# The two mixers of a fused two-block model: own normalised copy of x dropped, attention spread between the convolution's projections

## The chip, the cores and the metric

One core of a Trainium2 chip runs the whole model. The metric is the time of one execution in microseconds on the device. The engines named below are TensorE (PE), VectorE (DVE), ScalarE (ACT), GpSimd (POOL) and SyncE (SP), which issues most DMAs.

## The reference, cut to what matters

x is 256 tokens by 1024 channels, all in float32. The model runs eleven stages: mixer, mixture of experts, mixer, mixture of experts, a norm, two feed-forward stages with a pooling mixer between, a feed-forward stage, a sparse-attention mixer ("nsa") and a last feed-forward stage. Only the two mixers change. Each computes:

```
h    = rmsnorm(x, norm_mix)
proj = h @ w_in                      # 1024 -> 512 q, 128 k, 128 v, 512 gate_b, 512 gate_c, 512 u
q, k = partial_rope(q), partial_rope(k)                  # 8 query heads, 2 key/value heads, width 64
y_attn = windowed_gqa_with_sink(q, k, v, sink)           # keys with |i-j| <= 128, one sink logit per head
y_conv = gate_b * centred_short_conv(gate_c * u, conv_w) # 3 taps over the tokens
y = concat(rmsnorm(y_attn, g_attn), rmsnorm(y_conv, g_conv))
x = x + y @ w_out
```

## The kernel before

All engines run one hand-written program; the order of the work is the order of the statements, and semaphores join the engines. The weights stream through a ring of six 2 MB buffers in SBUF. SP issues the loads in the order in which they are used, and each waits until its buffer's last user has signalled. A mixer uses seven buffers (five column blocks of `w_in`, two row blocks of `w_out`), and the ring then fills with the first six expert matrices. In the expert stage a load is issued when the pair of experts before has been multiplied (L516).

A mixer on PE (`mixer`, from L771): turn the normalised `hp` into `hT` (`transpose_h`, L693) and wait for all of it; q, k and v with tokens on the partitions (`tokens_out`, L704); gate_c, u and gate_b with channels on the partitions (`channels_out`, L718), 96 matmuls in a row; turn q and k (L783, L786); then four attention units, two blocks of 128 queries by two key/value heads, in `attend`: scores of 4 heads by 256 keys (L731), turning the probabilities (L743), the product with V (L754), where the turned probabilities are the stationary operand and 64 columns of V move. Then the sums of squares of the convolution's output (L795), its half of the out-projection (L814), turning the attention's output (L803), and the other half (L814).

ACT takes results from PSUM (`copy`, L1240), takes the exponentials (L1327) and the roots. DVE normalises x into `hp` (`norm`, L1647), rotates q and k (L1714 to L1718), makes the convolution (L1785 to L1800), adds the window's mask to the scores in SBUF (L1730), takes their maximum (L1732) and three small steps (L1738 to L1742), scales each head's output (L1807), and adds the two halves to x (L1821). In the nsa stage the kernel already has an attention with the mask added on PE (L1130), two heads of a pair on the two halves of the rows (L1135), probabilities scaled by DVE before they are turned (L2153, L1150), and V stationary (L1160).

Of the kernel before, what the change touches and what calls it, by code (L numbers as in the profile page):

```python
# [14 lines left out]
P = 128  # L15
# [30 lines left out]
for _n, _w in (("ident", P), ("upper", P), ("ones", P), ("fold", CAP), ("iota", CAP), ("tie", NG + NE), ("rope_c", TT * ROPE),  # L46
               ("rope_s", TT * ROPE), ("band", TT * SEQ), ("causal", P), ("cmp_mask", TT * NCMP), ("cmp_any", TT)):
    CONSTS[_n] = (_at, _at + _w)
    _at += _w
# [3 lines left out]
def constants():  # L53
# [20 lines left out]
    keys = np.arange(SEQ)  # L74
    put("band", np.where(np.abs(keys[None, None, :] - tok[:, :, None]) <= 128, 0.0, -BIG))
# [15 lines left out]


class Unit:


    def __init__(self, t, g, half, gp, tile, br, nk, qT, kT, v, mask):
        self.t, self.g, self.half, self.gp, self.tile, self.br, self.nk = t, g, half, gp, tile, br, nk
        self.qT, self.kT, self.v, self.mask = qT, kT, v, mask
# [39 lines left out]
def build(nc, a, out, stages):  # L138
    ctx = ExitStack()
    with ctx:  # L140
# [54 lines left out]
        r_query = small[:, 28:30]  # L195

# [41 lines left out]
        S.masked = sem("masked")  # L238
# [3 lines left out]
        S.turned_taken = sem("turned_taken")  # L242
        S.valued = sem("valued")
        S.o_taken = sem("o_taken")
        S.conv_gain = sem("conv_gain")
        S.conv_ss = sem("conv_ss")
        S.conv_root = sem("conv_root")
        S.ya_root = sem("ya_root")
        S.ya_psum = sem("ya_psum")
        S.yaT_ready = sem("yaT_ready")  # L250
        S.acc_done = sem("acc_done")
# [69 lines left out]
        def mixer_views():  # L321
            c = Carve()
            b = Fields()
            b.q, b.kv = c(TT, 512), c(TT, 256)
            b.v = b.kv[:, :, P:256]
            b.qT, b.kT = c(4, SEQ), c(1, SEQ)
            b.ya, b.yc = c(TT, 512), c(4, SEQ)
            b.tmp = c(256)
            b.stat = c(4, 16)
            b.z = c(4, SEQ + 2)  # L330
            b.P = [c(4, SEQ) for _ in range(2)]
            b.Sm = [c(4, SEQ) for _ in range(2)]
            b.PT = [c(2, 4, P) for _ in range(2)]
            b.sq = hp[:, 0, :].rearrange("p (a b) -> p a b", a=4)
            b.gate_c = hp[:, 1, :].rearrange("p (a b) -> p a b", a=4)
            b.cv = b.P[0]
            b.yaT = b.Sm[0]
            b.junk = b.Sm[1]
            return b
# [83 lines left out]
        def mixer_units():  # L423
            return [Unit(t=t, g=g, half=g, gp=0, tile=0, br=0, nk=2, qT=MB.qT, kT=MB.kT, v=MB.v,
                                    mask=const("band")[:, t * SEQ:(t + 1) * SEQ])
                    for t in range(TT) for g in range(2)]
# [40 lines left out]
        def _(sp):  # L467
# [153 lines left out]
        def _(pool):  # L621
# [6 lines left out]
            with nc.allow_non_contiguous_dma(reason="small parameters, transposed"):  # L628
# [8 lines left out]
                par(gT[:, 0, :], a["norm_mix"][0].rearrange("(p k) -> p k", k=KT), True)  # L637
# [8 lines left out]
                par(gT[:, 1, :], a["norm_mix"][1].rearrange("(p k) -> p k", k=KT))  # L646
# [26 lines left out]
        def _(pe):  # L673
# [25 lines left out]
            def tokens_out(r, width, banks, offs=(0, 0), each=True):  # L699

                wv = view(r, KT, width)
                for t in range(TT):
                    for k in range(KT):
                        last = pe.matmul(PS[:, banks[t], offs[t]:offs[t] + width], hT[:, k, t * P:(t + 1) * P],  # L704
                                         wv[:, k, :], start=(k == 0), stop=(k == KT - 1))
                    if each:
                        last.then_inc(S.projected, 1)
                if not each:
                    last.then_inc(S.projected, 1)

            def channels_out(r, banks):

                wv = view(r, KT, 512)
                for c in range(4):
                    if c == 2 and banks[1] == 4:
                        pe.wait_ge(S.act_took, w.to(S.act_took))
                    for k in range(KT):
                        last = pe.matmul(PS[:, banks[c // 2], (c % 2) * SEQ:(c % 2 + 1) * SEQ],  # L718
# [5 lines left out]
            def attend(units, b):  # L724
                def scores(i):
                    u = units[i]
                    if i >= 2:
                        pe.wait_ge(S.masked, w.to(S.masked))
                    lo = DH * u.half
                    for r in range(4):  # L730
                        last = pe.matmul(PS[:, 2 * (i % 2) + r // 2, (r % 2) * SEQ:(r % 2) * SEQ + u.nk * P],  # L731
                                         u.qT[lo:lo + DH, u.tile + r, u.t * P:(u.t + 1) * P],
                                         u.kT[lo:lo + DH, u.gp, 0:u.nk * P], start=True, stop=True)
                    last.then_inc(S.scored, 1)

                def turn(i):
                    u = units[i]
                    pe.wait_ge(S.exped, w.to(S.exped))
                    if i:
                        pe.wait_ge(S.turned_taken, w.to(S.turned_taken))  # L740
                    for kt in range(u.nk):
                        for r in range(4):
                            last = pe.transpose(PS[:, 4 + kt, r * P:(r + 1) * P],  # L743
                                                b.P[i % 2][:, r, kt * P:(kt + 1) * P], ident)
                    last.then_inc(S.turned, 1)

                def values(i):
                    u = units[i]
                    if i >= 2:
                        pe.wait_ge(S.o_taken, w.to(S.o_taken))  # L750
                    for r in range(4):
                        lo = r * DH
                        for kt in range(u.nk):
                            last = pe.matmul(PS[:, 6 + i % 2, lo:lo + DH], b.PT[i % 2][:, kt, r, :],  # L754
                                             u.v[:, kt, u.g * DH:(u.g + 1) * DH],
                                             start=(kt == 0), stop=(kt == u.nk - 1))
                    last.then_inc(S.valued, 1)

                scores(0)
                for i in range(len(units)):  # L760
                    if i + 1 < len(units):
                        scores(i + 1)
                    turn(i)
                    if i:
                        values(i - 1)
                pe.wait_ge(S.turned_taken, w.to(S.turned_taken))
                values(len(units) - 1)
                pe.wait_ge(S.masked, w.to(S.masked, 2))
                pe.wait_ge(S.o_taken, w.to(S.o_taken, 2))

            def mixer(l):  # L771
                transpose_h()
# [1494 lines left out]
```

## Time and profile before

| | us |
|---|---|
| three runs | 2336.04, 4395.04, 2329.59; median 2336.04 |
| the profiled execution | 2328.93, of which the trace spans 2327.1 |
| PE busy | 2145.3 (92%) |
| DVE busy, ACT busy | 767.1 (33%), 630.8 (27%) |
| chain that ended last | PE 65%, DMA 27%, DVE 5%, ACT 2% |

The profile's page gives each engine's busy time and follows back the chain of work that ended last; the trace behind it gives every instruction. The two mixers lie at about 9 to 164 us and 665 to 822 us of the span. Busy time of PE is modelled and holds short matmuls' fill, so it isn't a share of PE's peak. A float32 matmul stands as two instructions in the trace (x64 for 32 matmuls of L704); a transpose is one.

### The profile page before, as it was taken

To read this page: it belongs to the slowest core of one execution; us is meant where nothing else is said; L and a number is where in the kernel's file an instruction comes from. 1 tells how busy PE (TensorE), PEld (TensorE's weight loads), DVE (VectorE), ACT (ScalarE), POOL (GpSimd) and SP (SyncE) were. 2 spreads that over 40 slices of the span, in tenths; PEclk is the share of its full clock that TensorE was granted. 3 is DMA by queue.
4 is the path that set the end of the run, shared out by engine and by line. 5 is a ranking of instruction groups with operands and counts; after the bars stand their busy time and mean duration, and the time that the engine had idled before them with its cause. 6 is when DMAs were issued, how large, how long until landed. Compare 5 with 4: busy or idle time off the path is not lost.

```text
span 2327.1 us, 28410 instructions
## 1 busy us (share of the span) xinstructions
PE 2145.3 (92%) x11998; PEld 1469.0 (63%) x11998; DVE 767.1 (33%) x1119; ACT 630.8 (27%) x886; POOL 35.9 (2%) x53
## 2 busy tenths in 40 slices
PE   6889999999978989999999799989999999999998
PEld 4755443444437644444444499969998995566997
DVE  1321111111112221111111365555556553274555
ACT  1221111111111211111111333343344332264333
POOL 5000000000000000000000000000000000000000
PEclk9879999999989789999999899989999999999999
DMA  9326999999964149999999955354455435513430
GB/s 282 156 72 266 421 422 421 422 421 422 422 242 175 36 171 422 421 422 421 423 422 421 395 181 181 114 209 164 174 201 203 162 130 176 179 56 144 167 125 36
DMA packets 142459, 599.18 MB, mean 257 GB/s; under 512 B 6913, under 2 KB 22337, under 8 KB 126002
## 3 DMA queue, kind: packets, MB, share of 16 engines
q1 hardware_dynamic: 139730, 592.27, 65.1%
q0 software_dynamic: 2656, 5.86, 1.0%
q8 instruction: 55, 0.90, 0.2%
q14 instruction: 18, 0.15, 0.0%
HBM read 597.06 MB, written 1.05 MB: 257 GB/s over the span
## 4 chain that ended last, share of the span: by engine, by line
PE 65%; DMA 27%; DVE 5%; ACT 2%; issue 1%; SPq 0%; DVEq 0%; ACTq 0%
DMA ring<-in_w_expert_up 26%; PE PS L972 20%; PE PS L848 12%; PE PS L986 10%; PE PS L718 4%; PE PS L1059 3%; PE PS L814 3%; PE PS L959 2%; PE PS L704 2%; PE PS L859 1%; PE PS L1212 1%; PE PS L837 1%; PE PS L754 1%; DMA ring<-in_w_in 1%; PE PS L731 1%
## 5 line engine op out<-in xcount | busy, mean ns | idle before, releaser
L848 PE MATMUL PS<-ring,xs 128*64 128x512 f32 x2048 | 465.6, 609 | 57.1 <-DMA ring<-in_w_expert_up 55.7
L848 PEld LDWEIGHTS PS<-ring,xs 128*64 128x64 f32 x2048 | 159.8, 140 | 356.3 <-issue 353.3
L1240 ACT ACTIVATE split<-ring 128x2048 fp32r<-128x2048 f32 x132 | 253.1, 1920 | 424.2 <-PE PS L972 268.0
L1693 DVE TENSOR_TENSOR split<-ring,split 128x2048 fp32r<-128x2048 f32 x132 | 302.3, 2293 | 176.9 <-ACT split L1240 171.7
L972 PE MATMUL PS<-hT_high,split 128*128 128x256 f32 x2560 | 329.1, 281 | 0.0
L972 PEld LDWEIGHTS PS<-hT_high,split 128*128 128x128 f32 x2560 | 316.5, 189 | 2.8
L986 PE MATMUL PS<-split,ffn_hid 128*128 128x512 f32 x1056 | 246.9, 390 | 0.0
L859 PE MATMUL PS<-ring,work 128*64 128x512 f32 x1024 | 226.8, 595 | 0.0
L986 PEld LDWEIGHTS PS<-split,ffn_hid 128*128 128x128 f32 x1056 | 195.5, 188 | 39.0
L972 PE MATMUL PS<-hT_low,split 128*128 128x256 f32 x1280 | 178.3, 282 | 0.0
L1240 ACT ACTIVATE work<-PS 128x512 f32<-128x512 f32 (+1 forms) x73 | 47.4, 656 | 439.5 <-PE PS L884 326.6
L972 PEld LDWEIGHTS PS<-hT_low,split 128*128 128x128 f32 x1280 | 163.6, 189 | 0.0
L1854 DVE SCALAR_TENSOR_TENSOR y_low<-PS,work,y_high 128x1024 fp32r<-128x1024 f32 x32 | 41.1, 1284 | 353.7 <-ACT y_high L1393 353.7
L1849 DVE TENSOR_TENSOR work<-PS,work 128x512 f32<-128x512 f32 x32 | 22.1, 691 | 410.8 <-PE PS L848 410.8
L859 PEld LDWEIGHTS PS<-ring,work 128*64 128x64 f32 x1024 | 70.7, 137 | 131.8 <-issue 127.9
L837 PE MATMUL PS<-work,hp 128*128 128x128 f32 x1088 | 132.6, 282 | 3.0 <-DVE work L1831 3.0
L837 PEld LDWEIGHTS PS<-work,hp 128*128 128x128 f32 x1088 | 129.6, 199 | 3.2 <-issue 3.2
L1393 ACT ACTIVATE y_high<-PS,work 128x1024 fp32r<-128x1024 f32 x32 | 35.6, 1113 | 207.7 <-PE PS L859 207.7
L718 PE MATMUL PS<-hT,ring 128*128 128x256 f32 x384 | 83.2, 379 | 0.0
L718 PEld LDWEIGHTS PS<-hT,ring 128*128 128x128 f32 x384 | 73.0, 190 | 9.9
L1240 ACT ACTIVATE xs<-PS 128x512 f32<-128x512 f32 x68 | 40.6, 597 | 130.0 <-PE PS L837 130.0
L1059 PE MATMUL PS<-ring,hT 128*128 128x512 f32 (+1 forms) x192 | 72.9, 539 | 0.4 <-ACT hT L1501 0.4
(265 smaller groups left out, 1680.3 us busy)
## 6 DMA issues: line engine op xcount, KB each, us to landing
ring<-in_w_expert_gate SPq DMA_DIRECT2D x64, 2048.0 KB, 17.4
ring<-in_w_expert_up SPq DMA_DIRECT2D x64, 2048.0 KB, 17.7
ring<-in_w_expert_down SPq DMA_DIRECT2D x64, 2048.0 KB, 14.4
ring<-in_ffn_w_gate SPq DMA_DIRECT2D x20, 2048.0 KB, 8.7
ring<-in_ffn_w_up SPq DMA_DIRECT2D x20, 2048.0 KB, 9.1
ring<-in_ffn_w_down SPq DMA_DIRECT2D x20, 2048.0 KB, 7.9
ring<-in_w_in SPq DMA_DIRECT2D x8, 2048.0 KB, 18.9
ring<-in_nsa_w_in SPq DMA_DIRECT2D x5, 2048.0 KB, 7.9
```

Source lines behind the costliest of these rows:

```text
L704: last = pe.matmul(PS[:, banks[t], offs[t]:offs[t] + width], hT[:, k, t * P:(t + 1) * P], wv[:, k, :], start=(k == 0), stop=(k == KT - 1))
L718: last = pe.matmul(PS[:, banks[c // 2], (c % 2) * SEQ:(c % 2 + 1) * SEQ], wv[:, k, c * P:(c + 1) * P], hT[:, k, :], start=(k == 0), stop=( ...
L814: last = pe.matmul(PS[:, 4 * part + 2 * t + h, :], src[:, c, t * P:(t + 1) * P], wv[:, c, h * 512:(h + 1) * 512], start=(c == 0), stop=(c ...
L837: last = pe.matmul(PS[:, 6 + b, (k % 4) * P:(k % 4 + 1) * P], hp[:, t, k * P:(k + 1) * P], EB.OH[:, t, :], start=(t == 0), stop=(t == 1))
L848: last = pe.matmul(PS[e * CAP:(e + 1) * CAP, bank, :], xs[:, k, e * CAP:(e + 1) * CAP], view((r + e) % RING, KT, DE)[:, k, :], start=(k == ...
L859: last = pe.matmul(PS[e * CAP:(e + 1) * CAP, 6 + c, :], EB.hT[:, k, e * CAP:(e + 1) * CAP], view((r + e) % RING, 4, D)[:, k, c * 512:(c + ...
L959: last = pe.matmul(PS[:, 2 * (kind == "up") + ft, 0:SEQ], split_cols(0, kind, part)[:, k, ft * P:(ft + 1) * P], hx[:, k, :], start=(n_ == ...
L972: last = pe.matmul(PS[:, bank, ft * SEQ:(ft + 1) * SEQ], split_cols(b, kind, part)[:, k, ft * P:(ft + 1) * P], hx[:, k, :], start=(n_ == 0 ...
L986: last = pe.matmul(PS[:, 2 * t + c, :], ffn_hid[:, b % 2, hpart, ft, t * P:(t + 1) * P], wv[:, ft, c * 512:(c + 1) * 512], start=(b == 0 a ...
L1059: last = pe.matmul(PS[:, banks[t], offs[t]:offs[t] + width], hT[:, k, t * P:(t + 1) * P], wv[:, k, :], start=(k == 0), stop=(k == KT - 1))
L1240: return act.activation(o, i, ACT.Copy)
L1693: v.tensor_tensor(at[:, 1], src, at[:, 0], ALU.subtract).then_inc(S.ffn_low, 1)
```

## The change

- No normalised copy: PE turns x itself (`transpose_x`, which the expert stage has too, here with its line in the first mixer waiting for the load of x), hT holds x times the gain, and the root of the mean square comes in later: as a scale when ACT takes q, k and v, as a broadcast row `r2` (two matmuls of a diagonal with ones) on gate_c, and as one factor of the convolution's norm. u and gate_b are left without it.
- `w_in` is read with channels k*128+p on partition p instead of 8p+k, and `norm_mix` likewise. The mask table leaves the constants (512 of 1284 columns). 
- The first projection starts when the first two channel blocks of hT are there.
- k is taken twice, so that two query heads of a pair lie on the upper and lower 64 partitions; the mask comes from PE as a product of an identity with a triangle that opens the sum; the scale 1/8 is in q.
- Probabilities are divided by their sum on DVE before they are turned; ACT and DVE each take one half of the turned ones; V is stationary, and the output comes out turned, [64 x head, queries], straight usable by the out-projection. Its gain is applied when ACT takes it. The turning of the attention's output is gone.
- PE's order is new: the attention's units stand between the channel blocks of u and gate_b, and the out-projection is four pieces of 8 matmuls. The last ring slots of `w_out` are given back at the third and fourth piece.

The instructions that compute 4 sums of squares (L768 in the new program) are 16 matmuls instead of 8.

On PE, between the projection of k and v and the out-projection, before:

```order
L718 MATMUL PS<-hT,ring 128x256 x96
L783 MATMUL PS<-cst,work 128x128 x8
L786 MATMUL PS<-cst,work 128x128 x2
L731 MATMUL PS<-work 128x256 x8
L743 MATMUL PS<-cst,work 128x128 x8
L731 MATMUL PS<-work 128x256 x4
L743 MATMUL PS<-cst,work 128x128 x8
L754 MATMUL PS<-work 128x64 x8
```

And on the same engine in the changed program, from the second half of gate_c on (L723 channel blocks, L736 mask, L740 scores, L750 turning, L762 values):

```order
L723 MATMUL PS<-hT,ring 128x256 x16
L736 MATMUL PS<-causal_r,ident_r 128x2x128 x2
L740 MATMUL PS<-work 128x256 x4
L723 MATMUL PS<-hT,ring 128x256 x16
L750 MATMUL PS<-cst,work 128x128 x8
L736 MATMUL PS<-causal_r,ident_r 128x2x128 x2
L740 MATMUL PS<-work 128x256 x4
L723 MATMUL PS<-hT,ring 128x256 x8
L762 MATMUL PS<-work 64x256 x4
L723 MATMUL PS<-hT,ring 128x256 x8
L750 MATMUL PS<-cst,work 128x128 x8
```

All 96 channel matmuls stood ahead of the first score; now 64 of them stand between a unit's scores and its turning, 16 for each unit.

On DVE in the changed program, unit 1 with the work that stands around it (L1826 maximum, L1810 and L1815 convolution, L1843 scaling of the probabilities, L1804 the product gate_c*u, L1848 half of the turned probabilities):

```order
L1826 TENSOR_REDUCE work<-PS 128x4
L1829 TENSOR_TENSOR work<-work 128x4
L1832 TENSOR_TENSOR work<-work,sink 128x4
L1810 TENSOR_SCALAR work<-work,cw 128x256 x2
L1815 SCALAR_TENSOR_TENSOR work<-work,cw 128x256 x4
L1839 TENSOR_TENSOR work<-work 128x4
L1663 RECIPROCAL work<-work 128x4
L1843 TENSOR_TENSOR work<-work 128x1024
L1804 TENSOR_TENSOR work<-PS,work 128x2x256
L1848 COPY work<-PS 128x512
```

The convolution stood ahead of the attention; now half of it stands between the maximum and the scaling of units 1 and 2.

At the end of the mixer on PE, in the changed program (L774 out-projection, L768 sums of squares):

```order
L750 MATMUL PS<-cst,work 128x128 x8
L774 MATMUL PS<-ring,work 128x512 x8
L762 MATMUL PS<-work 64x256 x4
L768 MATMUL PS<-cst,work 128x1 x12
L774 MATMUL PS<-ring,work 128x512 x8
L768 MATMUL PS<-cst,work 128x1 x4
L774 MATMUL PS<-ring,work 128x512 x16
```

Before, 16 matmuls of L814, the 8 transposes of L803 and 16 of L814 stood there; the first piece now runs ahead of the last unit's values.

The diff, cut to the parts that the prediction speaks of:

```diff
@@ def mixer_loads(l) (SP)
-                    wide(wi, lo, hi, S.projected, k)
-                rows(a["w_out"][l], 512, 1024, S.acc_done, 1)
-                rows(a["w_out"][l], 0, 512, S.y_done, TT)
+                    wide(wi, lo, hi, S.projected, k, "(k p) n -> p k n")
+                rows(a["w_out"][l], 512, 1024, S.y_done, 3)
+                rows(a["w_out"][l], 0, 512, S.y_done, 1)
@@ PE
+            def mixer(l):
...
+                def scores(i):
+                    t, g = units[i]
+                    if i:
+                        pe.wait_ge(S.exped, w.to(S.exped))
+                    for h in range(2):
+                        other = PS[:, h, :].rearrange("p (s k) -> p s k", s=2)[:, :, (1 - t) * P:(2 - t) * P]
+                        kept, moved = (causal_r, ident_r) if t else (ident_r, causal_r)
+                        pe.matmul(other, kept[:, :], moved[:, :].unsqueeze(1).to_broadcast([P, 2, P]),
+                                  start=True, stop=False, skip_group_check=True)
+                    for s_ in range(2):
+                        for h in range(2):
+                            last = pe.matmul(PS[:, h, s_ * SEQ:(s_ + 1) * SEQ],
+                                             MB.qT[DH * h:DH * (h + 1), 2 * g + s_, t * P:(t + 1) * P],
+                                             MB.kT[DH * h:DH * (h + 1), g, :],
+                                             start=False, stop=True, skip_group_check=True)
+                    last.then_inc(S.scored, 1)
...
+                def values(i):
+                    t, g = units[i]
+                    pe.wait_ge(S.turned_act, w.to(S.turned_act))
+                    pe.wait_ge(S.turned_dve, w.to(S.turned_dve))
+                    if i >= 2:
+                        pe.wait_ge(S.oT_taken, w.to(S.oT_taken))
+                    for kt in range(TT):
+                        for h in range(2):
+                            last = pe.matmul(PS[DH * h:DH * (h + 1), 6 + g, 0:SEQ], MB.v[:, kt, g * DH:(g + 1) * DH],
+                                             MB.PT[i % 2][:, kt, 2 * h:2 * h + 2, :], start=(kt == 0), stop=(kt == 1))
+                    last.then_inc(S.oT_done, 1)
...
+                transpose_x(f"mix{l}", 4)
+                project(512, (0, 1), first=True)
+                project(256, (2, 2), (0, 256))
+                pe.wait_ge(S.diag_made, w.to(S.diag_made))
+                for t in range(TT):
+                    last = pe.matmul(PS[:, 6, t * P:(t + 1) * P], ones, MB.sF[:, t, :], start=True, stop=True)
+                last.then_inc(S.r_wide, 1)
+                wv = view(slot(), KT, 512)
+                channels(wv, 3, 0)
+                channels(wv, 3, 1)
+                pe.wait_ge(S.q_roped, w.to(S.q_roped, 3))
...
+                scores(0)
+                wv = view(slot(), KT, 512)
+                pe.wait_ge(S.gated, w.to(S.gated))
+                channels(wv, 3, 0)
+                channels(wv, 3, 1)
+                turn(0)
+                scores(1)
+                pe.wait_ge(S.gated, w.to(S.gated))
+                channels(wv, 2, 2)
+                pe.wait_ge(S.r_taken, w.to(S.r_taken))
+                values(0)
+                channels(wv, 2, 3)
+                turn(1)
+                scores(2)
...
+                rows_out(MB.oT, attn_w, 0, 0)
+                values(3)
+                pe.wait_ge(S.yc_gain, w.to(S.yc_gain, 2))
+                for t in range(TT):
+                    sum_squares(PS[:, 4, t:t + 1], MB.sqc, t)
+                sum_squares(PS[:, 4, 2:3], MB.sqa, 0).then_inc(S.mix_ss, 1)
+                rows_out(MB.yg, conv_w, 0, 2)
+                pe.wait_ge(S.oT_taken, w.to(S.oT_taken, 2))
+                sum_squares(PS[:, 5, 0:1], MB.sqa, 1).then_inc(S.mix_ss, 1)
+                rows_out(MB.yg, conv_w, 1, 6)
+                pe.wait_ge(S.mix_root, w.to(S.mix_root, 2))
+                rows_out(MB.oT, attn_w, 1, 4)
@@ ACT
+                exps(0)
+                for i in range(3):
+                    take(i)
+                    exps(i + 1)
+                    outputs(i)
+                table_for_roots()
+                conv_gain(0)
+                take(3)
+                conv_gain(1)
+                outputs(3)
```

## Rows read from the trace of the kernel before

**Rows 1.** Chain of waits, first mixer: start us, us, what
```profile
1.74 19.82 DMA ring<-in_w_in
21.70 22.46 PE PS L704 x64
44.16 41.44 PE PS L718 x192
...
126.85 3.55 PE PS L795 x16
130.40 15.75 PE PS L814 x32
...
148.24 14.02 PE PS L814 x32
162.35 1.29 DVE x L1821
```

**Rows 2.** Busy us by stretch: PE, PEld, DVE, ACT, POOL, granted clock, DMA share, GB/s
```profile
60.00:80.00 20.00, 20.00 (x94) 17.62 (x93) 7.36 (x15) 0.00 (x0) 0.00 (x0) 1.00 0.76 306
100.00:120.00 20.00, 18.84 (x75) 16.49 (x73) 7.40 (x16) 6.96 (x21) 0.00 (x0) 0.50 0.01 1
```

**Rows 3.** SP's issues in order of time, end of the first mixer
```profile
146.18 16.47 SPq L482 DMA_DIRECT2D ring<-in_w_expert_down  x2
194.29 0.92 SPq L516 DMA_DIRECT2D ring<-in_w_expert_gate  x2
```

**Rows 4.** Chain of waits, end of the first expert stage and second mixer
```profile
613.72 22.15 DMA ring<-in_w_expert_up
...
662.82 2.37 DVE x L1869 x2
...
681.42 20.88 PE PS L704 x64
...
806.49 14.02 PE PS L814 x32
```

**Rows 5.** PE in order of time, start of the second mixer and of ffn00
```profile
672.53 0.69 PE L693 MATMUL PS<-cst,hp 128*128 128x128 f32 x2 [9.75 <-issue]
677.18 3.22 PE L693 MATMUL PS<-cst,hp 128*128 128x128 f32 x14 [3.96 <-issue]
...
1329.49 3.67 PE L826 MATMUL PS<-cst,x 128*128 128x128 f32 x16 [9.49 <-DVE x L2232]
```

**Rows 6.** DMA queues from 669 to 670 us: packets, MB, share
```profile
q8 instruction: 1, 0.02, 7.1%
```

**Rows 7.** Instructions in order of time, first mixer
```profile
107.07 3.78 PE L731 MATMUL PS<-work 64*128 64x256 f32 x8
112.15 1.22 DVE L1732 TENSOR_REDUCE work<-work 128x4 f32<-128x1024 f32 x1
113.60 0.17 DVE L1740 TENSOR_SCALAR work<-work 128x4 f32<-128x4 f32 x1
...
145.99 1.04 PE L803 MATMUL PS<-cst,work 128*128 128x128 f32 x8
```

**Rows 8.** Groups by line and shape, first mixer: busy us, mean ns, idle before
```profile
L1327 ACT ACTIVATE work<-work 128x256 f32<-128x256 f32 x16 | 7.9, 493 | 0.0
L1795 DVE SCALAR_TENSOR_TENSOR work<-work,cw 128x256 f32<-128x256 f32 x8 | 3.9, 484 | 0.3
```

**Rows 9.** Instructions in order of time, nsa stage
```profile
2055.53 0.48 PE L1130 MATMUL PS<-causal_r,ident_r 128*128 128x256 f32 x2
2055.94 0.71 PE L1135 MATMUL PS<-work 64*128 64x128 f32 x8
...
2059.42 0.65 PE L1160 MATMUL PS<-work 128*64 128x256 f32 x4
```

**Rows 10.** Groups by line and shape, nsa stage
```profile
L2153 DVE TENSOR_TENSOR work<-work 128x1024 f32<-128x1024 f32 x8 | 9.8, 1224 | 0.3
```

**Rows 11.** Busy us by stretch, nsa attention (columns as in rows 2)
```profile
2050.00:2070.00 20.00, 20.00 (x146) 13.13 (x146) 13.01 (x28) 16.57 (x73) 0.00 (x0) 0.94 0.00 1
```

More of the change, by code:

```diff
@@ L423, in mixer_units, with mixer_scores @@
         def mixer_units():
[L424 to L426 removed]
+            return [(t, g) for t in range(TT) for g in range(2)]
+        def mixer_scores():
+            return PS[:, 0:2, :].rearrange("p h (s k) -> p (h s) k", s=2)
         def nsa_units():
@@ L697, in transpose_h @@
                 pe.wait_ge(S.hT_odd, w.to(S.hT_odd, 2))
[L699 to L718, printed above, removed]
-                                         wv[:, k, c * P:(c + 1) * P], hT[:, k, :],
-                                         start=(k == 0), stop=(k == KT - 1))
-                    if c % 2:
-                        last.then_inc(S.projected, 1)
@@ L724, in attend @@
[L724 to L769, printed above, removed]
@@ L1240, in copy @@
                 return act.activation(o, i, ACT.Copy)
-            def squares(src, junk, sums):
-                for t in range(TT):
-                    last = act.activation(junk(t), src(t), ACT.Square, accum_out=sums[:, t:t + 1])
-                last.then_inc(S.act_step, 1)
-                act.wait_ge(S.act_step, w.to(S.act_step))
             def roots(o, i, width, s):
@@ new lines, in take, with outputs @@
+                    copy(MB.PT[i % 2][:, 0, :, :].rearrange("p r q -> p (r q)"), PS[:, 4, :]).then_inc(S.turned_act, 1)
+                def outputs(i):
+                    t, g = units[i]
+                    act.wait_ge(S.oT_done, w.to(S.oT_done))
+                    o = PS[:, 6 + g, 0:SEQ].rearrange("p (s q) -> p s q", s=2)
+                    act.activation(MB.sqa[:, 2 * g:2 * g + 2, t * P:(t + 1) * P], o, ACT.Square)
+                    for s_ in range(2):
+                        m = 2 * g + s_
+                        last = act.activation(MB.oT[:, m, t * P:(t + 1) * P], o[:, s_, :], ACT.Copy, scale=gaT[:, l, m:m + 1])
+                    last.then_inc(S.oT_taken, 1)
@@ new lines, in conv_gain @@
+                def conv_gain(half):
+                    act.wait_ge(S.yc_made, w.to(S.yc_made))
+                    act.activation(MB.sqc[:, 2 * half:2 * half + 2, :], MB.yc[:, 2 * half:2 * half + 2, :], ACT.Square)
+                    for c in range(2 * half, 2 * half + 2):
+                        last = act.activation(MB.yg[:, c, :], MB.yc[:, c, :], ACT.Copy, scale=gcT[:, l, c:c + 1])
+                    last.then_inc(S.yc_gain, 1)
+                exps(0)
[3 more added lines that the diff above has]
+                    outputs(i)
@@ L1377, in experts @@
+                roots(root_mix[:, 3:4], PS[:, 5, 0:1], 512, S.mix_root)
             def experts(s, f, passes, y_high):
@@ L1771, in mixer @@
+                for t in range(TT):
+                    last = v.tensor_scalar(MB.sF[:, t, :], ident, rstd[:, t:t + 1], rstd[:, t:t + 1], ALU.mult, ALU.mult)
+                last.then_inc(S.diag_made, 1)
                 for t in range(TT):
```

480 lines of the change are left out of this document (257 added, 223 removed).

## Prediction, made before the changed kernel ran

> **What bounds the kernel now.** I read the chain of waits first. In the first mixer it is PE almost without a break: it waits for the first block of `w_in` until 21.6 us, projects q, k and v in 22.46 us, runs 96 channel matmuls in 41.44, and ends with two halves of the out-projection, 15.75 and 14.02 us [rows 1]. The second mixer has the same chain from 681.42 to 820.51 us [rows 4]. Between the last channel matmul (85.60 us) and the out-projection (130.40) lie 44.8 us of attention and sums of squares. Here the stretches show what is wrong: the granted clock is 1.00 in the projections and 0.50 from 100 to 120 us, although PE counts as busy for 18.84 of 20 us there [rows 2]. So attention costs twice: PE waits for DVE and ACT between a unit's scores and its turning, and its matmuls then run at 1.2 instead of 2.4 GHz.
>
> Does time saved in a mixer reach the end? The expert stage between is bound by its loads (one of 22.15 us is a link of the chain [rows 4]), and a stage bound by DMA can swallow a gain on PE. But its steady loading begins at 194.29 us, 30.6 us after x is ready at 163.64, since it waits for the first pair of experts to be multiplied [rows 1, 3], and in the mixer's late part DMA is idle (share 0.01 [rows 2]). An earlier x shifts that whole stream, so the gain carries over one for one.
>
> **The change, part by part.** I sum the PE work of the changed mixer from its first projection to its last matmul, at full clock.
>
> - q, k, v: unchanged, 20.88 us (second mixer [rows 4]; 22.46 in the first, where PE starts from idle [rows 1]).
> - 96 channel matmuls, only moved: 41.44 us [rows 1]. Out-projection, unchanged in size: 2 x 14.02 = 28.0.
> - 12 transposes of q and k: 8 took 1.04 us [rows 7], so 1.6. The two matmuls for `r2`, four instructions of that width: 0.5.
> - Sums of squares, now 16 matmuls of one column. Before, 8 took 3.55 us [rows 1] just before the out-projection still began slow. At full clock I take half of that each: 3.6 for 16. Upper bound 7.1.
> - One unit: mask 0.48; scores 8 instructions of 128 columns in 0.71 us in nsa, where the two heads of a pair lie on different rows of PE, so 1.4 for 256 columns (upper bound 1.9, half of the 3.78 us that this mixer's unpaired scores took at half clock); turning 1.04; values 0.65 for half of them, so 1.3 [rows 7, 9]. Together 4.2, four units 16.8.
>
> The sum is 20.9 + 41.4 + 28.0 + 1.6 + 0.5 + 3.6 + 16.8 = 112.8 us, and 1.6 more in the first mixer. Before, that stretch was 140.6 us (21.70 to 162.26) and 139.1 us. Gain: 26.2 and 26.3 us.
>
> This holds if PE does not wait for a unit's softmax. What must fit under the channel matmuls: maximum 1.22, two small steps 0.34, then on DVE half of the convolution, four steps of 0.48 and two shorter, some 2.6, in which ACT takes its four exponentials (4 x 0.49 and 0.2), then two small steps 0.35 and the scaling 1.22: 5.8 us [rows 7, 8, 10]. PE has 16 channel matmuls there, 41.44 / 6 = 6.9 us, and for units 1 to 3 another 1.3 of values. The cover is thin for unit 0, but that one has no convolution in its way (5.3 us). Each later unit has over 2 us to spare. If the cover were gone, a unit would expose the whole 5.8.
>
> ACT's copies of q, k and v with a scale and the rotation of the now doubled k lie under the first eight gate_c blocks (6.9 us). Square and gain of the convolution, the last take and the table of roots on ACT lie under the first out-projection piece (7.0 us), where only the last unit's take is waited for. DVE's adds lie under the later pieces; the last one, 1.29 us, stays exposed as before [rows 1]. So these cost nothing; with the cover gone they are at most some 4 us a mixer. The two last ring buffers return later relative to the end (at the third and fourth piece instead of halves one and two). They feed the first pair's down matrices, and the first pair's gate loads are used up only 30.6 us after x, so there is room for two loads.
>
> Front of the first mixer: it stays bound by the load of `w_in`. Norm, transposes and hT are done ahead of it before and now. The constants shrink by 512 of 1284 columns, 256 KB ahead of that load, at the first stretch's pace about 1 us; the new row order of `w_in` keeps pieces of 2 KB. I take 0.8 (0 to 1.2). The parameters' gather of `norm_mix` in single floats could take some of it back.
>
> Front of the second mixer: here a norm of both row blocks, transposes of `hp` and a wait for all of hT disappear, and x is ready at 665.19 while the projection starts at 681.42 [rows 4]. In ffn00, which turns x itself, 16 transposes take 3.67 us, and the first products follow at once [rows 5]. That would give a start at about 668, a gain of 13 us. But PE did not stand still for data alone: it ran two transposes at 672.53, stopped for 3.96 us with nothing to wait for, and ran on at 677.18 [rows 5], and a packet of instructions was brought in at 669 to 670 us [rows 6], just after the branch over the unused expert code. If both stops remain in time, the 14 last transposes end at 680.4 and the gain is 1.0; if only the first, the projection starts at about 676.4 and it is 5. I take 3, with 0 and 13 as the ends.
>
> The Trainium skill (Runtime: NRT & Kernel Launch, "Instruction fetch mechanics") says that a taken branch to code outside the resident pages must wait for a DMA fetch. By that rule the stops belong to the jump and not to the norm, which agrees with the row on the packet; without it the sum would have 10 us more gain.
>
> **Sum:** 26.2 + 26.3 + 0.8 + 3 = 56.3 us off the profiled 2328.93: 2272.6. The profiled execution lies 7 us under the shown median (2336.04) and 0.7 under the lowest run, so I put the median at 2272.
>
> **The rivals.**
>
> *A. The softmax is exposed.* DVE and ACT answer later than PE works through 16 channel matmuls. Before, they were exposed in every unit, which speaks for it; the sum of 5.8 under 6.9 to 8.2 us speaks against, and so does nsa, where the same pieces keep PE at 20.00 of 20 us [rows 11]. All four units exposed in both mixers cost 8 x 5.8 = 46 us: 2319.
>
> *B. The clock stays down, and the kernel gets slower.* The stretch at 0.50 had PE counted busy for 94% [rows 2], so short matmuls with many weight loads do not by themselves bring the clock back. If the mixture of units and channel blocks is seen like that, it is the dense work that pays: from the first scores to the end PE has 16.8 + 27.6 + 3.6 + 28.0 = 76 us a mixer. At half clock that is 152 us more in all, 96 net: 2425. If the clock came back at the out-projection it would be 89 us more, 32 net: 2361. The gain is gone at 28 us a mixer at 1.2 GHz; slower by 2% needs 52 of the 76. Against it: nsa's attention, with turned probabilities, paired heads and V stationary, had 0.94 [rows 11], and 64 dense channel matmuls now stand between.
>
> The Trainium skill (TensorE: Matmul & The Clock Gate, "A second HAM failure mode: psum-queue depth-cycling") describes a kernel that rests briefly between groups while it cycles through PSUM banks and whose clock swings between both levels. The nsa row does not bear that out for these pieces, and no row shows it for this mixture.
>
> *C. The front of the second mixer gains all of it:* 13 instead of 3, 2262.
>
> *D. The gain doesn't arrive,* because the expert stage's loads set its end whatever x does: both mixers' gains but the front's would have to be hidden in it, and I have found no row for it: about 2325.
>
> **Chances.** A measurement of this kernel can tell about 2% (47 us, 2289) from no change. Forecast 0.71, C 0.11, A 0.10 in full or in most part, B 0.05 (0.03 at 2425), D 0.03. The forecast's own range is 2262 to 2284: unknown prices are 3.5 us a mixer for the sums of squares, 2 for the scores, a few us of handovers, and the front. For 8 in 10 I reach from C's 2257 to a part of A, 2292. Faster by over 2%: forecast, C and a piece of A, 0.84. Within 2%: 0.12. Slower by over 2%: 0.04.
>
> **What would show each step.** The chain in a mixer should be channel, mask, score and value matmuls on PE with no DVE or ACT link over 1 us between. The granted clock from the first projection to the last matmul should be near 1.00. The out-projection should be four pieces of 7.0 us. From the first projection to the last matmul it should be 111 to 118 us. The steady expert loads should begin near 163 us. A stop "issue" on PE at the second mixer's first transposes should remain. I am wrong if PE waits for the scaled probabilities by more than 2 us a unit, if the clock shows 0.5 to 0.8 between, or if the expert stages, 501 us from x to x, change length.

## The result and the profile after

The changed kernel took 2272.56 us (median of four, 2270.97 to 2273.72), the kernel before 2332.82 on the same chip: a ratio of 0.9754 with an interval of 0.9737 to 0.9770, faster by 2.5%. One of the four executions of the kernel before took 4395.04 us, and the ratio leaves it out, so it stands for 57 us where the two medians lie 60 apart. The forecast was 2272, and the profiled execution took 2272.86, with a span of 2271.0 against 2327.1. The spans differ by 56.1 us; the prediction's sum had 56.3.

The chain of waits in the first mixer after (start us, us, what). It answers to [rows 1].

```profile
60.56 0.23 PE PS L736 x2
60.79 1.06 PE PS L740 x8
61.86 7.10 PE PS L723 x32
68.96 0.87 PE PS L750 x8
...
100.44 0.87 PE PS L750 x8
101.31 6.87 PE PS L774 x16
108.18 1.01 PE PS L762 x8
109.19 2.77 PE PS L768 x24
111.96 8.67 PE PS L774 x16
120.63 0.79 PE PS L768 x8
121.42 13.86 PE PS L774 x32
```

All of it is PE: mask (L736), scores (L740), channel matmuls (L723), turning (L750), values (L762), sums of squares (L768), out-projection (L774). Where 44.8 us of attention stood before, no DVE or ACT link is left. The chain at the start of the second mixer after answers to [rows 4, 5]:

```profile
635.24 2.37 DVE x L1936 x2
...
638.59 6.22 issue
644.81 2.82 PE PS L697 x12
647.63 1.83 issue
649.46 0.66 PE PS L697 x4
```

and the same chain at the end of that mixer:

```profile
734.97 3.28 PE PS L768 x24
738.25 9.83 PE PS L774 x16
748.08 0.79 PE PS L768 x8
748.87 13.86 PE PS L774 x32
```

The norm, the transposes of `hp` and the wait for hT are gone, but the two stops of [rows 5] are there again: PE waits 6.22 and 1.83 us with nothing that the profile shows. Last, the stretches after (busy us of PE, PEld, DVE, ACT and POOL, granted clock, DMA share, GB/s), to be held against [rows 2]:

```profile
80.00:100.00 20.00, 20.00 (x110) 15.70 (x109) 10.84 (x22) 9.29 (x30) 0.00 (x0) 1.00 0.29 106
100.00:120.00 20.00, 20.00 (x74) 10.62 (x73) 3.00 (x5) 4.12 (x12) 0.00 (x0) 0.91 0.29 105
740.00:760.00 20.00, 20.00 (x50) 9.21 (x49) 3.48 (x4) 1.41 (x3) 0.00 (x0) 0.90 0.15 43
```

PE is busy for all 20 us of each, and the clock is 1.00 while units and channel blocks alternate (also from 60 to 80 us). Between the first projection and the last matmul it falls only at the sums of squares (109.19 and 734.97): it is 0.57 from 112 to 116 us, just behind them, and 0.84 from 735 to 738, while they run.

**Where the 56.1 us came from.** From the first projection to the last matmul it is 114.1 us in the first mixer (21.16 to 135.28) and 112.6 in the second (650.12 to 762.73), against 140.6 and 139.1: 26.5 us each. The first mixer starts 0.5 us earlier. In the second, the way from x to the projection fell from 16.2 to 12.5 us (637.61 to 650.12): 3.7. Those make 57.2. The expert stage between took 500.95 us from x to x against 501.55, so it passed on everything and 0.6 more, 57.8 us in all at the last add of the second mixer (764.11 against 821.89); its steady loads follow x, now at 166.6 us instead of 194.29 [rows 3]. The issues after, by line and operation (ns shortest/median/longest, first and last start in us):

```profile
L506 SPq DMA_DIRECT2D ring<-in_w_expert_gate x8: 345/346/363, 166.6 to 248.8; - x8
```

At the end of the second expert stage the kernel was 57.1 us ahead (1322.41 against 1265.32), at the end of the span 56.1; I did not follow these last 1.7 us.

### The profile page after: what moved, and what is told of

Same layout as the page of the kernel before. It is cut to its first block, busy times and chain, and to the rows that moved or that the text cites. A ratio compares the mean times of both kernels' runs of the same rounds, so it can differ in the third digit from the quotient of the medians.

```text
span 2271.0 us, 28397 instructions
## 1 busy us (share of the span) xinstructions
PE 2110.4 (93%) x11978; PEld 1432.7 (63%) x11978; DVE 769.3 (34%) x1125; ACT 628.4 (28%) x902; POOL 35.7 (2%) x53
## 4 chain that ended last, share of the span: by engine, by line
PE 65%; DMA 28%; DVE 4%; issue 1%; ACT 1%; SPq 0%; DVEq 0%; ACTq 0%
DMA ring<-in_w_expert_up 27%; PE PS L987 20%; PE PS L863 12%; PE PS L1001 10%; PE PS L723 4%; PE PS L1074 3%; PE PS L774 3%; PE PS L974 2%; PE PS L713 2%; PE PS L874 1%; PE PS L1227 1%; PE PS L852 1%; DMA ring<-in_w_in 1%; DVE x L1701 1%; PE PS L697 1%
## 5 line engine op out<-in xcount | busy, mean ns | idle before, releaser
L1921 DVE SCALAR_TENSOR_TENSOR y_low<-PS,work,y_high 128x1024 fp32r<-128x1024 f32 x32 | 41.1, 1284 | 353.7 <-ACT y_high L1425 353.7
L1255 ACT ACTIVATE work<-PS 128x512 f32<-128x512 f32 (+1 forms) x65 | 40.0, 619 | 370.5 <-PE PS L899 325.2
L723 PE MATMUL PS<-hT,ring 128*128 128x256 f32 x384 | 87.3, 383 | 0.0
L723 PEld LDWEIGHTS PS<-hT,ring 128*128 128x128 f32 x384 | 71.5, 190 | 14.0 <-issue 5.0
## 6 DMA issues: line engine op xcount, KB each, us to landing
ring<-in_w_expert_gate SPq DMA_DIRECT2D x64, 2048.0 KB, 17.4
```

Of the source, the lines that this page charges most:

```text
L723: last = pe.matmul(PS[:, bank, (c % 2) * SEQ:(c % 2 + 1) * SEQ], wv[:, k, c * P:(c + 1) * P], hT[:, k, :], start=(k == 0), stop=(k == KT - 1))
L1255: return act.activation(o, i, ACT.Copy)
```

## The experiments

There were three theories: (1) most of the gain is PE working through channel blocks while DVE and ACT do a unit's softmax, and the granted clock staying up with it; (2) what is left at the second mixer's start is the fetch of code behind the branch over the unused expert code; (3) the slow out-projection piece comes from the one-column matmuls ahead of it. The kernel before, on the chips of these runs, lay between 2328.47 and 2332.95 us, so small differences are read from traces or on one chip.

**e1: the units after the channel blocks.** The change's pieces are all kept, but the four units no longer alternate with the blocks. ACT and DVE are reordered to match.

```diff
-                scores(0)
...
-                turn(0)
-                scores(1)
...
-                values(0)
...
+                scores(0)
+                pe.wait_ge(S.yc_made, w.to(S.yc_made, 2))
+                for i in range(4):
+                    if i + 1 < 4:
+                        scores(i + 1)
+                    turn(i)
+                    if i:
+                        values(i - 1)
+                values(3)
```

> The changed kernel with its cheap attention units, but all 96 channel matmuls ahead of the first score, and the units in the old two-deep order (next scores, turn, values of the one before); ACT and DVE reordered to match. Theory (half of the gain or more is the spreading: it hides the softmax and keeps the clock up): the granted clock falls to about 0.5 in the attention, a unit takes 6 to 7 us instead of 3.2, the sums of squares double; some 22 us more a mixer, about 2317. Rival (the gain comes from the dropped work: no copy of x, paired heads, V stationary, no turning of the output; order is worth little): at most 5 us a mixer, 2282 or less.

Measured: 2303.5 us, ratio 0.9874 (0.9854 to 0.9894), against 0.9754 for the change. Its chain in the first mixer:

```profile
87.30 1.24 DVE work L1833
...
89.16 1.83 ACT work L1368 x8
...
91.42 1.24 DVE work L1850
...
92.70 1.97 PE PS L753 x8
...
95.10 2.03 PE PS L740 x8
```

and its stretches:

```profile
80.00:100.00 20.00, 13.16 (x66) 10.25 (x64) 8.66 (x17) 5.74 (x25) 0.00 (x0) 0.80 0.30 106
100.00:120.00 20.00, 15.94 (x72) 9.82 (x73) 6.89 (x13) 9.51 (x29) 0.00 (x0) 0.69 0.00 1
```

The DVE and ACT links are back on the chain, and turning (L753) takes 1.97 us instead of 0.87, since the clock is at its lower level there. The mixers last 128.9 and 130.0 us: 14.8 and 17.4 longer than after, 11.7 and 9.1 shorter than before. So alternation is worth about half of the gain: 28 of 57 us by the ratios, 32 of 53 by the mixers of these executions. Theory (some 2317) gave it too much and the rival (2282 or less) too little.

The first mixer's chain also parts the two prices. In one block the four units take 31.8 us (85.96 to 117.78) against 12.7 when they alternate, 19.1 more. PE's own links are 17.6 of the 31.8, so the lower clock is some 4.9 of the 19.1, and the other 14.2 are waits for DVE and ACT. Channel matmuls in one row, a faster first projection and faster out-projection pieces gave 4.3 us back.

The first mixer of e1 is 11.7 us shorter than that of the kernel before. The stretch from the first score to the last value fell from 38.4 us (87.49 to 125.88) to 31.8, the turning of the output (2.1) is gone, and the out-projection took 27.9 instead of 29.8. Those are 10.6 of the 11.7. The single pieces (mask on PE, row halves, stationary V) were not taken out one by one.

**e2: two score matmuls on the same rows of PE next to each other.** Does the price of the scores rest on the order in which the two halves are written?

```diff
-                    for s_ in range(2):
-                        for h in range(2):
+                    for h in range(2):
+                        for s_ in range(2):
```

> The four score matmuls of a unit in the order h, s instead of s, h, so that matmuls that follow each other use the same half of PE's rows. Theory (neighbouring heads on different row halves run beside each other): a unit's scores take 1.8 us instead of 1.06, all on PE's path, 8 x 0.75 = 6 us more, about 2278.5. Rival (PE pairs them whatever the order, or the pair does not overlap): no change, 2272.5.

Measured: 2272.82 us, ratio 0.9744 (0.9728 to 0.9761). The eight instructions took as long as before the edit:

```profile
58.02 1.07 PE PS L740 x8
```

The order is worth nothing. This does not show that the two halves are worth nothing: in both orders one unit's scores use both. At the lower clock these eight took 2.03 us in e1, and the old kernel's eight of the same shape, all four matmuls of a unit on one half of the rows, 3.78 [rows 7].

**e3: no branch.** The overflow body of the expert stage, which these inputs never need, is left out with its test on PE, ACT, DVE and SP.

```diff
-                pe.wait_ge(S.flag_ready, w.to(S.flag_ready))
                 pe.wait_ge(S.moe_added, w.to(S.moe_added))
-                most = pe.value_load(flag[0:1, l:l + 1], min_val=0, max_val=SEQ)
-                with pe.If(most > CAP):
-                    experts(OV[l], Follow(), MORE * PAIRS, y_high[l])
...
```

> Leaves out, on all engines, the read of the flag and the branch with the second expert passes behind it, which these inputs do not enter. Theory (the 6.22 us and 1.83 us in which PE stands at the second mixer's first transposes come from the jump over that code): PE starts them within 1 us of x, the first projection some 8 to 10 us earlier; in the norm after the second expert stage PE has other work to wait for, so little there; about 2262. Rival (PE stands there for another reason, such as the busy DMA queues or x itself): gain under 1.5 us, 2271 to 2272.

Measured: 2260.25 us, ratio 0.9692 (0.9676 to 0.9708). The chain at its second mixer:

```profile
637.31 2.82 PE PS L696 x16
640.13 21.51 PE PS L712 x64
```

The 16 transposes run at once, and the projection starts 3.1 us after x (636.99) instead of 12.5. Both stops went with the branch and the code behind it; together with what they cover they cost 9.4 us. The edit takes out both at once, so it does not say which of the two a stop belongs to; e4 and e7 do. The time fell by 12.3, and the difference is theory 3's: in this execution the second mixer's slow piece took 6.97 us instead of 9.83, and the sums ahead of it 2.77 instead of 3.28.

**e4: PE waits for the sums of x behind the branch.** Then the branch does not stand behind DVE's last adds.

```diff
-                pe.wait_ge(S.moe_added, w.to(S.moe_added))
+                added = w.to(S.moe_added)
                 most = pe.value_load(flag[0:1, l:l + 1], min_val=0, max_val=SEQ)
                 with pe.If(most > CAP):
+                    pe.wait_ge(S.moe_added, added)
                     experts(OV[l], Follow(), MORE * PAIRS, y_high[l])
```

> PE waits for the sums of the expert stage (the DVE adds, S.moe_added) inside the branch's fall-through path instead of ahead of the branch. Theory (the stop of 6.22 us at the second mixer is the fetch of the code behind the branch, and it starts only once PE has waited for the last add): the fetch starts some 2.4 us earlier, beside the last DVE link of 2.4 us, so the stop after x is ready is near 3.9 us instead of 6.22, the second mixer ends about 2.4 us earlier and the time is near 2270. Rival (the stop starts with the wait inside the new code, or the sequencer reaches the branch no earlier than x is ready): no change, 2272.5.

Measured: 2268.79 us, ratio 0.9735 (0.9718 to 0.9752), which overlaps the change's interval. In the profiled execution (2272.34 us) the pieces behind the sums of squares took 9.91 and 9.95 us, so a gain at the front would not show in its time. The chain decides:

```profile
637.09 2.37 DVE x L1937 x2
...
640.45 0.25 issue
640.70 2.82 PE PS L697 x12
643.52 3.21 issue
646.73 0.66 PE PS L697 x4
```

The first stop is gone under DVE's work: transposes start 1.2 us after x (639.46) instead of 7.2. Part of it came back at once, since the second stop grew from 1.83 to 3.21 us. From x to the projection it is 7.9 us, 4.6 less than after, twice the 2.4 that I expected. The queue that brings in instructions says why. Its packets, from 642 to 643 us after, then from 638 to 639 and from 644 to 645 us in e4:

```profile
q8 instruction: 1, 0.02, 6.7%
q8 instruction: 1, 0.02, 6.9%
q8 instruction: 1, 0.02, 7.3%
```

After, the first packet comes some 5 us behind x (637.61). In e4 it comes some 1 us ahead of x (639.46), so the fetch no longer waited for the adds. A second packet lies ahead of the end of each second stop too (from 646 to 647 us after, where PE goes on at 649.46), and e3 has none between 626 and 654 us. This is the row of [rows 6] again, and it bears out that both stops are fetches of code.

**e7: the same code, moved.** 30 or 64 waits, never executed, are written into the overflow body of the first expert stage.

```diff
                 with pe.If(most > CAP):
+                    if l == 0:
+                        for _ in range(30):
+                            pe.wait_ge(S.const_loaded, 16)
                     experts(OV[l], Follow(), MORE * PAIRS, y_high[l])
```

> 30 waits are written on PE into the overflow body of expert stage 0, which is never executed; all code of PE behind the branch moves to higher addresses. Nothing that is executed changes. Theory (the two stops of PE at the start of the second mixer, 6.22 us before the transposes and 1.83 us after 12 of them, lie where the fetch of code ends a piece of fixed size): the second stop comes at another transpose, not after the 12th, and the projection begins up to 2 us later or earlier than 650.12. Rival (the second stop is a wait on data or a semaphore): it stays after the 12th transpose, with the same 1.8 us.

> As e7_pad30, with 64 waits. Theory (fetch in pieces of fixed size): the second stop comes at a third place or is gone, and the projection begins at another time than in both others, some 1.5 us earlier than 650.12 if the stop is gone. Rival (data or a semaphore): the second stop stays after the 12th transpose, with 1.8 us.

The chains, with 30:

```profile
635.36 6.20 issue
641.55 1.11 PE PS L697 x4
642.67 3.43 issue
646.10 2.82 PE PS L697 x12
```

and with 64:

```profile
639.81 6.22 issue
646.02 3.67 PE PS L697 x16
```

Nothing that is executed differs, and the second stop comes after 4 transposes instead of 12, or not at all. It is no wait for data: its place depends on where the code lies. From x to the projection it is 14.6 and 10.9 us, against 12.5. The first stop is the same in all three, 6.20 to 6.22 us. The times of one execution each, 2273.83 and 2268.58 us, point the same way, but single times do not settle 2 us.

**e5: the sums over channel blocks on DVE.** PE keeps one one-column matmul per sum instead of four.

```diff
-                def sum_squares(to, src, t):
-                    for c in range(4):
-                        last = pe.matmul(to, src[:, c, t * P:(t + 1) * P], ones[:, 0:1], start=(c == 0), stop=(c == 3))
-                    return last
+                def sum_squares(to, which, t):
+                    return pe.matmul(to, MB.sr[:, which, t * P:(t + 1) * P], ones[:, 0:1], start=True, stop=True)
...
+                v.tensor_reduce(MB.sr[:, 1, 0:P], MB.sqa[:, :, 0:P].rearrange("p c q -> p q c"), AX_X, ALU.add)
```

> The squares are first added over the four channel blocks on DVE (three reductions, 1.2, 0.7 and 0.7 us, where DVE is idle), so that PE has 4 one-column matmuls a mixer instead of 16. Theory (the long run of one-column matmuls pulls the clock down, and the next out-projection piece pays for it: 8.67 and 9.83 us instead of 6.9): PE's sums go from 3.6 and 4.1 us to about 0.6, and that piece back to 6.9; 5 us in the first mixer, 6.5 in the second, and the fewer instructions may move the second mixer's stop of 1.83 us away; 2259 to 2262. Rival (the piece is slow for another reason): only the 3 and 3.5 us of the sums, 2266. Second rival (DVE's reductions come late and PE waits for them): 2270 or more.

Measured: 2259.12 us, ratio 0.9683 (0.9667 to 0.9699). The first mixer:

```profile
107.56 0.76 PE PS L769 x6
108.32 6.97 PE PS L774 x16
115.29 0.12 PE PS L769 x2
115.41 13.86 PE PS L774 x32
```

The sums cost 0.88 us instead of 3.56 and 4.07, the piece behind them 6.97 instead of 8.67 and 9.83: 10.4 us over both mixers. The spans differ by 12.7; 1.6 of the rest is an earlier end of the first projection (43.36 against 44.99), which starts with the load of `w_in` and is no part of the edit; 0.8 is the second mixer's start, where the moved code meets only one stop. DVE's three reductions cost nothing: no link of theirs is on the chain.

**e6 and e9: a quarter, and twice, of the one-column matmuls.** These separate the matmuls from DVE's part in e5. (The two texts count instructions; a matmul here is two, and there are 32 per mixer, 24 of them ahead of the slow piece: 8 and 64 in these kernels.)

```diff
                 def sum_squares(to, src, t):
-                    for c in range(4):
-                        last = pe.matmul(to, src[:, c, t * P:(t + 1) * P], ones[:, 0:1], start=(c == 0), stop=(c == 3))
+                    for c in range(1):
+                        last = pe.matmul(to, src[:, c, t * P:(t + 1) * P], ones[:, 0:1], start=True, stop=True)
                     return last
```

That is e6; e9 has `range(8)`, over the blocks `c % 4`.

> The sums of squares on PE are made over one of the four channel blocks alone (six one-column matmuls per mixer in place of 24, no work added on DVE); three quarters of each sum are left out. Theory (the 24 one-column matmuls cost 2.8 to 3.6 us themselves and, in some executions, leave the granted clock below 1.00 for the out-projection's next piece, 8.7 to 9.8 us instead of 6.97): the sums take about 0.9 us, every piece of the out-projection about 6.97, and the time is near 2259, as with the sums made on DVE. Rival (the slow piece comes from the work before or beside the sums, ACT's and DVE's, and DVE's making the sums only moved that): the sums take 0.9 but a piece of 8.7 remains, near 2266.

> Each sum of squares on PE is made twice over (48 one-column matmuls per mixer in place of 24, nothing else changed). Theory (the one-column matmuls and the clock after them): the sums take 3.6 us more in each mixer, and the out-projection's next piece is slow (8.7 to 9.8 us) in both mixers, so 7 to 10 us more than 2272.6: 2280 to 2283. Rival (only the count of instructions costs, the clock has nothing to do with it): the next pieces come out as before, and at most 7 us more, 2279 to 2280; other rival (the sums' time is hidden by a wait for the squares anyway): under 3 us more.

e6's whole time, 3716.35 us, says nothing on the question. Left-out squares change x, so the experts' load changes, and the trace holds 5120 instructions of the expert products instead of 2048; with the first expert stage unchanged, that is the second one's overflow body. Its mixers can be read, the first one here:

```profile
109.25 0.76 PE PS L768 x6
110.01 6.97 PE PS L774 x16
```

No slow piece in either mixer, with DVE left as it was: e5's gain came from the missing matmuls. e9 took 2279.02 us, ratio 0.9786 (0.9770 to 0.9803), just under the theory's 2280 and at the rival's 2279, so the time does not choose. Its first mixer does:

```profile
108.56 7.36 PE PS L768 x48
115.92 8.37 PE PS L775 x16
```

and the stretch around the sums:

```profile
110.00:120.00 10.00, 10.00 (x43) 7.73 (x44) 1.62 (x3) 0.75 (x3) 0.00 (x0) 0.66 0.01 2
```

Here the clock falls while the sums still run: 48 instructions take 7.36 us, well over double the 2.77 of 24, so the count alone is not the price. In the second mixer they took 5.83 us and the next piece 9.97. Over all traces the next piece was slow (8.37 to 10.02 us) in 2 of 2 mixers with 64 such instructions, in 10 of 14 with 32, and in none of 10 with 8. The 2 of 2 alone would say little beside 10 of 14; none of 10 is what shows it. The 14 fall into three kinds. Where the 24 instructions took 3.1 to 3.4 us, the piece took 9.7 to 10.0 (6 mixers). Where they took 2.6 to 2.8, it took 8.67 (4) or 6.97 (4). So the clock drops at different moments, now during the sums, now behind them, and sometimes not at all.

**e8, e10, e11: both improvements.** e8 is e5 with e4's edit.

> The sums over channel blocks for the norms made on DVE (as in e5_dve_sums, 2259.1) and PE's wait for the expert stage's sums moved behind the branch (as in e4_early_branch). Theory (the two gains lie in different places and add): 2259.1 less 2.4 = 2256.7, range 2254 to 2259. Rival (the early branch is worth nothing): 2259.

Measured: 2254.24 us, ratio 0.9683 (0.9670 to 0.9697), on another chip than e5 and with the same ratio. Since the ratios did not tell the two apart, both ran once more on one chip, where the kernel before took 2329.72.

> The kernel of e5_dve_sums again, to stand beside e8_sums_and_branch on one chip. Theory (PE's wait behind the branch brings the second mixer's projection 4.6 to 5.2 us nearer to x, and all of it reaches the end): this one is 4 to 6 us above the other. Rival (the traces' 5 us are given back later, as in a slower expert stage): both within 1 us.

> The kernel of e8_sums_and_branch again, on the chip of e10_sums_same_chip. Theory: 4 to 6 us below it. Rival: within 1 us of it.

Measured: e5's kernel 2261.87 us (2260.64 to 2263.56; ratio 0.9710, 0.9692 to 0.9728), e8's 2255.22 (2249.43 to 2256.51; ratio 0.9674, 0.9654 to 0.9694). The ratios' intervals touch; the times of five runs each do not, and the medians lie 6.6 us apart. The chain of the second of them:

```profile
634.97 1.77 issue
636.75 3.67 PE PS L699 x16
```

From x to the projection it took 6.4 us (633.98 to 640.42), e5's kernel 11.0 (631.56 to 642.58). The traces account for 4.6 of the 6.6. This kernel (e8 and e11) is the fastest of the study, 17 to 19 us below the change by the ratios (0.9683 and 0.9674 against 0.9754), and it leaves nothing out.

## Why the prediction was right

The steps held: alternation hid the softmax and kept the clock up, the expert stage passed the gain on, and PE still stopped at the second mixer. That the time came within 1 us of the forecast is luck: terms of 1 to 4 us were off in both directions.

**The mixer's sum held, partly by errors that cancel.** Forecast against the first and second mixer, from the chain:

- q, k, v: 22.5 and 20.9; measured 23.83 and 20.64.
- Channel matmuls: 41.4; measured 42.82 in both. Cut into pieces they cost more: 3.65 for 16 instructions, where 32 in one piece take 7.10 or 6.91.
- Transposes of q and k with `r2`: 2.1; measured 1.75.
- Four units: 16.8; measured 12.70, that is mask 0.94, scores 4.24, turning 3.48, values 4.04. This is the term that was mis-sized. I took 1.4 for a unit's scores from nsa's pairs and 1.9 as the upper end, but it was 1.06, and the mask 0.23 instead of 0.48; the single rows that I took from the list of instructions [rows 7, 9] overlap with their neighbours, while the chain counts each stretch once.
- Sums of squares: 3.6; measured 3.56 and 4.07.
- Out-projection: 28.0; measured 29.4 and 30.56. Here the forecast of four pieces of 7.0 us failed for one piece in each mixer, 8.67 and 9.83.

Together 114.1 and 112.6, against the 114.4 and 112.8 forecast; the units' 4.1 us too much paid for the rest.

**No softmax exposed (rival A).** The cover was as forecast, thinnest for unit 0. Its scaling on DVE in the first mixer (start us, us, engine, line, operation):

```profile
66.03 1.23 DVE L1843 TENSOR_TENSOR work<-work 128x1024 f32<-128x1024 f32 x1
```

It ends at 67.26, and PE asks for it at 68.96: 1.7 us to spare. Units 1 to 3 had 2.4, 2.6 and 2.9 us. e1 shows the other side, with these links on the chain.

**The clock (rival B) stayed up where it mattered,** 1.00 from 60 to 109 us. But I had counted on 1.00 to the last matmul, and that was wrong. The row that I used for the sums' price showed a slow piece behind them too (3.55 and then 15.75 instead of 14.02 [rows 1]). It could not say whose that was, since the clock was at 0.50 ahead of those sums already (from 120 to 130 us). In the changed kernel it is 1.00 ahead of them (100 to 109 us), and e5 and e6 show that the slow piece comes with the sums.

**The front of the first mixer** was forecast at 0.8 and came out at 0.5, but that is not resolved: with the same front, the first projection began between 19.50 (e2) and 22.49 us (e11).

**The front of the second mixer** gained 3.7 us (forecast 3, between 0 and 13). The 3 was a middle between 1.0 with both stops and 5 with one, and that it came so near is luck: both stops stayed, but the second was shorter, 1.83 us instead of 3.96, and e7 moved it by the place of the code alone. That the stops would stay in spite of the norm's removal was right, and e3, e4 and e7 show why: the first belongs to the branch, the second to the place of the code. Rival C, all 13 us, would have needed both gone; e3, with both gone, has its projection 3.1 us after x, 13.1 less than before. The Trainium skill (Runtime: NRT & Kernel Launch, "Instruction fetch mechanics") says that a taken branch to code outside the resident pages waits for a DMA fetch. The traces agree: PE stops for 6.2 us here and a packet of instructions comes in meanwhile (642 to 643 us). That the fetch can be started early and hidden, as in e4, is this case's own result.

**Nothing was swallowed (rival D).** 500.95 against 501.55 us from x to x, and the steady loads begin 29.9 us after x (136.66) as they began 30.6 after it before. My 163 us for their start was a slip: 194.29 less the forecast gain of 27.0 is 167.3, and it was 166.6.

## What to carry to other kernels

When another engine's latency sits between short matmul groups, count both of its prices, the wait and the lower clock behind it, and put independent dense matmuls between; here that was worth about half of the gain, most of it from the wait, and cheaper pieces and fronts the rest. After such a change look for what still stands alone on PE: a row of one-column matmuls, or a branch that waits for data it does not need, cost 4 to 6 us each place and were taken out without any new arithmetic on PE.

## What the runs showed of the hardware

- A run of 12 one-column matmuls (24 instructions, 2.6 to 3.4 us) left the granted clock below 1.00 behind it in 10 of 14 mixers, and not in the others, with the same code. The piece behind them then took 8.67 to 10.02 us instead of 6.97. Where the run itself took over 3 us, the piece took 9.7 to 10.0. With 3 such matmuls in the run the piece was never slow (10 mixers). What decides between the cases was not found, nor whether it is the one column or the number of short matmuls that matters.
- PE's first stop at the branch was 6.2 to 7.5 us in the changed kernel, e1, e2, e5, e6, e7, e9 and e10, and 0.25 to 1.85 us where the branch stood ahead of the wait for x (e4, e8, e11). A second one of 1.72 to 3.43 us moved with the code's place or vanished. A packet of instructions came in shortly ahead of the end of each stop. So identical instructions cost 10.9, 12.5 or 14.6 us from x to the projection.
- Eight score instructions of 256 columns took 1.06 us at 1.00 in either order of the row halves. At the lower clock they took 2.03, and 3.78 when all used the same half.
